# Moving dots with gathered rows of u from the one-hot weights into the search for best sums

## The reference, cut to what matters

```python
q = (xc @ wq).reshape(PEER_CHUNK, PEER_HEADS, 2, half)
s1 = jnp.einsum('chd,hnd->chn', q[:, :, 0], keys1)
s2 = jnp.einsum('chd,hnd->chn', q[:, :, 1], keys2)
v1, i1 = lax.top_k(s1, PEER_TOPK)
v2, i2 = lax.top_k(s2, PEER_TOPK)
cand = (v1[..., :, None] + v2[..., None, :]).reshape(...)
best, pos = lax.top_k(cand, PEER_TOPK)
eidx = jnp.take_along_axis(cidx, pos, axis=-1)
g = jax.nn.softmax(best, axis=-1)
a = jnp.einsum('chkd,cd->chk', u_tab[eidx], xc)
wgt = (jax.nn.gelu(a) * g)
return jnp.einsum('chk,chkd->cd', wgt, v_tab[eidx])
```

## Time and profile before

| | us |
|---|---|
| median of 3 runs | 3125.98 (3116.21 to 3127.22) |
| the profiled execution's own time | 3124.37 |
| its span, first to last instruction | 3122.5 |
| PE busy | 2800.0 (90%) |
| DVE busy | 1457.4 (47%) |
| ACT busy | 988.8 (32%) |
| POOL busy | 532.5 (17%) |
| DMA, mean | 194 GB/s |

### The profile page before, as it was taken

The page is one execution under the profiler, slowest core; times in us unless marked ns, Lnnn a source line. Parts: engine busy times, 40 slices in busy tenths (PEclk is TensorE's granted clock), DMA queues, the critical chain, the costliest instruction groups (busy, mean ns, idle before and its releaser), DMA issues.

```text
span 3122.5 us, 30980 instructions
## 1 busy us (share of the span) xinstructions
PE 2800.0 (90%) x12382; PEld 1894.8 (61%) x12382; DVE 1457.4 (47%) x2814; ACT 988.8 (32%) x1234; POOL 532.5 (17%) x427
## 2 busy tenths in 40 slices
PE   6799998677767899999997999988998999999998
PEld 4566653322233444444443899988888977777775
DVE  3334221221124343333322299998988544444444
ACT  4644401120003210044502244344444433333332
POOL 0100000000000000000000000043434335565550
PEclk9899999789878999999998999999999999999999
DMA  3443432799960110020102235479998889999993
GB/s 143 155 162 135 162 135 83 255 374 374 373 233 0 40 41 27 27 81 27 39 16 67 95 134 191 163 252 338 332 353 327 323 294 327 312 318 313 319 327 106
DMA packets 295915, 606.99 MB, mean 194 GB/s; under 512 B 16503, under 2 KB 157943, under 8 KB 285848
## 3 DMA queue, kind: packets, MB, share of 16 engines
q1 hardware_dynamic: 224864, 385.37, 35.8%
q0 software_dynamic: 44528, 154.69, 13.5%
q10 hardware_dynamic: 26376, 64.90, 5.5%
HBM read 534.13 MB, written 70.78 MB: 194 GB/s over the span
## 4 chain that ended last, share of the span: by engine, by line
PE 67%; DVE 14%; DMA 9%; SPq 4%; issue 3%; ACT 3%; POOL 0%; ACTq 0%; DVEq 0%
PE P L2223 6%; PE P L2224 6%; PE P L2225 6%; DMA ug<-in_ur,sparse 5%; SPq L2312 4%; PE P L2065 4%; DVE window L474 4%; PE P L1744 4%; PE P L1771 4%; PE P L2001 3%; PE P L2118 3%; PE P L2120 3%; PE P L2119 3%; DVE part L474 2%; PE P L1677 2%
## 5 line engine op out<-in xcount | busy, mean ns | idle before, releaser
L474 DVE TENSOR_TENSOR part<-raw,part 128x2048 fp32r<-128x2048 f32 x136 | 311.2, 2289 | 403.1 <-ACT part L1535 341.4
L2118 PE MATMUL P<-hr,part 128*128 128x384 f32 (+1 forms) x1152 | 413.8, 359 | 67.8 <-DVE part L474 67.6
L2238 POOL DMA_INDIRECT ug<-in_ur,sparse x128 | 179.2, 1400 | 1347.9 <-DVE window L482 975.2
L2119 PE MATMUL P<-hr,part 128*128 128x384 f32 (+1 forms) x1152 | 406.0, 352 | 0.0
L2120 PE MATMUL P<-hr,part 128*128 128x384 f32 (+1 forms) x1152 | 405.9, 352 | 0.0
L1535 ACT ACTIVATE part<-raw 128x2048 fp32r<-128x2048 f32 x136 | 260.5, 1916 | 287.5 <-PE P L2225 219.1
L2223 PE MATMUL P<-part,ge 128*128 128x512 f32 x768 | 302.9, 394 | 0.7 <-issue 0.7
L2224 PE MATMUL P<-part,ge 128*128 128x512 f32 x768 | 299.4, 390 | 0.0
L2225 PE MATMUL P<-part,ge 128*128 128x512 f32 x768 | 299.0, 389 | 0.0
L2118 PEld LDWEIGHTS P<-hr,part 128*128 128x128 f32 x1152 | 224.8, 195 | 81.0 <-DVE part L474 75.0
L2119 PEld LDWEIGHTS P<-hr,part 128*128 128x128 f32 x1152 | 224.5, 195 | 5.7
(11 more groups left out here) (307 smaller groups left out, 4219.2 us busy)
## 6 DMA issues: line engine op xcount, KB each, us to landing
raw<-in_u SPq DMA_DIRECT2D x64, 1024.0 KB
raw<-in_v SPq DMA_DIRECT2D x64, 1024.0 KB
W<-in_w_in SPq DMA_DIRECT2D x18, 2048.0 KB, 7.8
W<-in_ada_w SPq DMA_DIRECT2D x12, 2048.0 KB, 7.9
W<-in_w_gate SPq DMA_DIRECT2D x24, 1024.0 KB, 14.6
W<-in_w_up SPq DMA_DIRECT2D x24, 1024.0 KB, 16.6
a_scratch<-gt ACTq DMA_DIRECT2D x128, 192.0 KB
w_scratch<-window ACTq DMA_DIRECT2D x12, 2048.0 KB
```

Source lines behind the costliest of these rows:

```text
L474: return v.tensor_tensor(out=out_, in0=in0, in1=in1, op=op)
L2118: t.matmul(b, wh[:, k, js], HR[0][:, k, lo:S], start=k == 0, stop=False)
L2119: t.matmul(b, wh[:, k, js], HR[1][:, k, lo:S], start=False, stop=False)
L2238: return g.indirect_dma_start(out=dst, out_offset=None, in_=src, in_offset=bass.IndirectOffsetOnAxis(ap=idx, axis=0)).then_inc(sem_, 16)
```

## The change

One dot step in 0.6 is woven into the search, from six steps behind `("gt", 0)` on; the ratios of the products beside the search and of the dots beside the one-hot steps are smaller. Nothing else is changed; the lines behind it move down by two.

```diff
         dots = [("ud", k) for k in range(128)]
         turns = [x for n in range(64) for x in ([("wd", n // 16)] if n % 16 == 0 else []) + [("sv", n)]]
-        ORDER3 = [("sc", 0)] + interleave(best, ahead, 0.58)
+        known = best.index(("gt", 0)) + 6
+        best = best[:known] + interleave(best[known:], dots, 0.6)
+        ORDER3 = [("sc", 0)] + interleave(best, ahead, 0.56)
         for kind in behind.values():
             ORDER3 += [(kind, 3)] + [dots.pop(0) for _ in range(2)] + [ahead.pop(0)]
-        wg_steps = interleave([("wg", x, i) for x in range(48) for i in range(2)], dots, 1.26) + dots + [("sw",)]
+        wg_steps = interleave([("wg", x, i) for x in range(48) for i in range(2)], dots, 0.95) + dots + [("sw",)]
```

## The result

The changed kernel takes 3105.51 us in the median of seven runs (3100.87 to 3117.64), the kernel before 3125.98 (3116.21 to 3129.25). The ratio is 0.9942, with a 95% interval of 0.9924 to 0.9961, so 18 us less (12 to 24); the two medians are 20.5 us apart, and forecast were 15.1. The two profiled executions are 17.4 us apart (3106.92 and 3124.37).

The account below looks back on a forecast made before the run. VectorE was taken to carry the one-hot stage, delayed by DMA queues, with TensorE and VectorE nearly full in the search. Search +52.4 and one-hot stage -67.5 gave -15.1 us, so 3110.9 us predicted, range 3092 to 3133.

Parts of the forecast that it names:

- The search, +52.4 forecast: Search stage: TensorE bounds it, 63.3 us of moved products less its waits of 8.6, 0.9 and 1.4.
- the 10.9 us of TensorE's waits: Search: TensorE's waits of 8.6, 0.9 and 1.4 us, taken to vanish once TensorE is the slower engine.
- my bounds: Search growth: from +39.5 us if VectorE's work alone counts to +63.3 if all the slack of before stays.
- The one-hot stage, -67.5 forecast: One-hot stage: VectorE's 302.4 us of work plus 17 of waits make 319.4, against 386.9 before.
- my lower end: One-hot stage: 8 us of waits, if the DMA engines' 282 us of work reach 0.91 of the stage again.
- the upper end, 26: One-hot stage: 26 us of waits for rows, if each of the 91 dots left waits as long as before.
- my own case: Both stages: waits of 8 to 26 us, search +47 to +58, total -24 to -6 us; chance 0.45.
- Rival A: One-hot stage: DMA queues stay full and 26 to 35 us of waits remain; sum -1.1, about 3125 us; chance 0.22.
- Rival B: Both stages: search only +45 us and 8 us of waits in the one-hot stage; sum -31.5, 3094 us; chance 0.22.
- Rival C: One-hot stage: idle TensorE drops to a lower clock and bounds the stage; sum +24.6, 3151 us; chance 0.05.
- Rival D: Search: the 29 moved gathers hold VectorE up for 33 us; sum +5.0, 3131 us; chance 0.06.
- the gain was not the moved work: Whole kernel: the gain is the waits for gathers that go, less VectorE's new idling in the search, not 49 or 63 us.

Follow-up runs that it names:

- dots_only: The changed kernel with 56 products before the one-hot steps instead of 71, the 37 dots kept; ratio 0.9903 against the kernel before.
- after_depth3: The changed kernel with one gather less in flight, same order and bytes; ratio 1.0070 against the kernel before.
- products_only: The kernel before with 71 products before the one-hot steps instead of 56, its 8 dots kept; ratio 1.0151 against the kernel before.
- weighted_quarters: Last run: the changed kernel with products spread by time (61 before the one-hot steps) and weight stores in four pieces; 3078.03 us, ratio 0.9855 against the kernel before.

## Why the prediction was right, and where by luck

- **The sign and the place.** The sum was -15.1 and came out at -17.4 in the profiled executions: longer search, shorter one-hot stage, by VectorE's work and the waits for gathered rows. That held, and `dots_only` and `after_depth3` show it.
- **Its own signs.** Most of what the prediction said would show it right did not come. The first one-hot instruction was to come near 2117 and came at 2128.0, behind the 2127 from which the prediction called itself wrong outside its cases. TensorE's waits for low halves were to fall under 8.6 us and were 12.3. The DMA share was to be at or under 0.90 and was 0.92, and the one-hot stage was 307.1 us with 5.3 of waits where 319 with 17 were forecast. Only VectorE's waits for high halves (23.6, above 7.3), the dots, no longer than before, and the tail, to 1.1 us, came as said.
- **The search, +52.4 forecast, +64.2 measured.** The prices held: 15 x 4.22 = 63.3, and TensorE is busy 62.1 us longer. The step that failed is the 10.9 us of TensorE's waits that I took off, since "with TensorE the slower one, the low halves should be there when it comes". They are 13.2 us afterwards instead. VectorE does run ahead in the light steps, but only by the two buffers, and the heavy steps use this up. So the upper end of my bounds, +63.3, was the value, and the time lay just outside it.
- **The one-hot stage, -67.5 forecast, -79.8 measured.** VectorE's work was forecast at 302.4 us, and 301.2 are busy in 307.1. TensorE's was forecast at 262.3, and it is busy 271.3, which did not matter here. The term that was mis-sized is the wait for rows: 17, as the middle of 8 and 26, where 5.3 us are left, below my lower end. That end came from a DMA share of 0.91 as a ceiling. It is none: the share is 0.92 here and 0.98 in the last experiment. My lower end had the wrong variable, load instead of lead; the upper end, 26, took it that each dot waits as long as before, and left out that the dots stand further apart.
- **The two errors are 12 us each and cancel.** That the total came within some us of the forecast is luck; the terms were each outside the bounds of my own case.
- **Rival A** (queues stay full) had its premise: they did stay full, at 0.92. The waits went all the same.
- **Rival B** had the waits about right (8 us) and the search wrong: +45 us were not to be had with 71 products, since TensorE alone is busy 319.9 us there, 51.9 more than the whole search lasted before.
- **Rival C** (TensorE's clock) took it that TensorE would be idle for 18% of the one-hot stage. It was for 12%, hardly more than the 11% before, so this run does not test its condition. The mean granted clock rose from 0.94 to 0.98. TensorE's pauses add up to 34.9 us in 23 pieces (25.2 of them for low halves), and only two are longer than 2.9 us, of 3.4 and 4.6; before they were 43.2 us in 18 pieces, with six of 3.0 to 5.2. `products_only` comes nearer to the condition, with TensorE busy for 295.3 of 378.3 us and single waits of over 10 us, and there the clock was 0.88. Even so VectorE's work and waits fill that stage. The rival asked that TensorE bound the stage, and it did in neither.
- **Rival D** (gathers hold VectorE up): with gathers all through the search the 128 dots last 1202 to 1233 ns, as before, and VectorE is busy 300.2 us where 252.5 + 49.1 = 301.6 follow. No block shows. The exclusion that the Trainium skill states in "SBUF — State Buffer", "Who interferes with whom", is one with a GpSimd instruction that reads SBUF. Whether issuing this indirect gather counts as such a read no run here settles; if it does, the trace does not agree.
- **That the gain was not the moved work** held, but I missed that the move of the products is a loss in itself: a product moved costs the search 4.22 us where TensorE bounds it, and saves the one-hot stage only VectorE's 1.14. `products_only` bears this out: for 15 products the search grew by 61.6 us, 4.1 each, and VectorE's busy time in the one-hot stage fell by 15.5, 1.0 each. I had both prices and never set them against each other.

## What to carry to other kernels

When a change moves two kinds of work, cost each kind by the engine that bounds the stage it leaves and the one it enters; here one half brought 30 us and the other gave 12 back. Compare the lead of a transfer (transfers in flight times the time between uses) with the time that it needs beside the largest burst; the DMA share does not tell, for here 41.5 us of waits stood at a share of 0.85 and 0.7 at 0.98. Where two engines go in step through a double buffer, try weaving their work by duration and not by number of steps; here it brought 6 us.

## What the runs showed of the hardware that was not expected

The 16 DMA engines were busy 0.98 of 312 us at 357 GB/s, with gathers of 4 KB rows, loads and stores mixed (`weighted_quarters`), and no wait of a computing engine for a transfer was longer than 0.7 us. I had read 0.91 as near to their limit. With the stores of 2 MB issued in one piece VectorE waited 34.4 us for gathered rows, and in four pieces, one after each of four one-hot steps, 18.9, with the same bytes.
